# A 512-token, two-block transformer kernel: the first block's mixer run in two passes, tiles 0 and 1 ahead of the expert gather, tiles 2 and 3 between the gathered rows

## The reference, cut to what matters

```python
# first block
hn = rms_norm(h, norm_mix_g);  proj = hn @ w_in          # xv, bg, cg, ga, gg, 512 columns each
y_sc = bg * causal_conv(cg * xv, w[3])                   # 3 taps
y_cf = silu(layer_norm(causal_conv(ga * sigmoid(gg), w[31]) + b, ln_g, ln_b))   # 31 taps
h = h + concat(rms_norm(y_sc), rms_norm(y_cf)) @ w_out
hn = rms_norm(h, norm_ffn_g)
q = hn @ w_q                                             # 8 heads x 2 halves x 128
s1, s2 = q halves @ sub_keys;  top 16 of each, top 16 of their 256 sums -> idx, gates
u_sel = u[idx];  v_sel = v[idx]                          # 8 heads x 16 = 128 rows a token
h = rms_norm(h + sum(gelu(u_sel . hn) * gates * v_sel))
# second block: x = x + ffn1; x = x + attention mix; x = x + ffn2
```

## Time and profile before

| | |
|---|---|
| time, median of 3 runs | 2445.37 us (2444.99 to 2446.51) |
| span of the profiled execution, first to last instruction | 2440.3 us |
| busy share: PE, DVE, ACT, POOL | 87%, 75%, 48%, 31% |
| mean granted TensorE clock | 0.940 |
| moved by DMA | 760.89 MB, mean 312 GB/s |
| first and last gather issued | 243.09 us, 1807.03 us |

### The profile page before, as it was taken

The page is one execution under the profiler, slowest core; times in us unless marked ns, Lnnn a source line. Parts: engine busy times, 40 slices in busy tenths (PEclk is TensorE's granted clock), DMA queues, the critical chain, the costliest instruction groups (busy, mean ns, idle before and its releaser), DMA issues. The chain is left out here.

```text
span 2440.3 us, 28668 instructions
## 1 busy us (share of the span) xinstructions
PE 2117.7 (87%) x9528; PEld 1505.2 (62%) x9528; DVE 1829.9 (75%) x3369; ACT 1180.3 (48%) x3781; POOL 751.1 (31%) x634
## 2 busy tenths in 40 slices
PE   6987898897777776999784688699989999999999
PEld 6966444343222223885343467388539988898997
DVE  6985686777988888989889988866675656656664
ACT  5213556555666665343455555433344446445443
POOL 0000445445554554233456544433320001100000
PEclk9988899999999998999896679799999999999999
DMA  5211999999999999999999999999986444224454
GB/s 200 86 52 52 377 417 414 422 404 421 419 421 421 416 420 369 390 405 420 417 402 368 377 406 420 416 403 420 421 343 207 177 175 161 75 99 156 177 187 138
DMA packets 107460, 760.89 MB, mean 312 GB/s; under 512 B 12064, under 2 KB 12832, under 8 KB 16432
## 3 DMA queue, kind: packets, MB, share of 16 engines
q0 software_dynamic: 73728, 536.90, 53.9%
q1 hardware_dynamic: 33584, 222.15, 23.9%
HBM read 756.91 MB, written 2.10 MB: 311 GB/s over the span
## 5 line engine op out<-in xcount | busy, mean ns | idle before, releaser
L2448 POOL DMA_INDIRECT pair<-in_uv,idx x512 | 639.6, 1249 | 850.3 <-DVE resid L1079 519.5
L1837 ACT ACTIVATE smalls<-smalls 128x1 f32<-128x1 f32 (+1 forms) x2058 | 540.1, 286 | 640.5 <-DVE smalls L1747 622.3
L1747 DVE CUSTOM_DVE_ANT_0 pair<-pair,hn 128x1024 f32<-128x1024 f32 x512 | 624.2, 1221 | 179.8 <-DMA pair<-in_uv,idx 178.4
L596 PE MATMUL bank<-pair,diag 128*128 128x512 f32 x928 | 452.3, 619 | 124.5 <-ACT diag L1837 124.3
L596 PEld LDWEIGHTS bank<-pair,diag 128*128 128x128 f32 x928 | 167.3, 192 | 389.9 <-ACT diag L1837 243.9
L596 PE MATMUL bank<-ft,raw 128*128 128x256 f32 x1664 | 375.4, 389 | 11.9 <-DVE ft L1073 11.9
L596 PEld LDWEIGHTS bank<-ft,raw 128*128 128x128 f32 x1664 | 324.6, 196 | 58.7 <-issue 12.7
L1079 DVE SCALAR_TENSOR_TENSOR resid<-pair,smalls,resid 128x1024 f32<-128x1024 f32 x275 | 352.4, 1281 | 0.6 <-ACT smalls L1837 0.6
L1073 DVE TENSOR_TENSOR half<-raw,half 128x1024 fp32r<-128x1024 f32 (+1 forms) x204 | 235.6, 1194 | 124.6 <-ACT half L1837 123.2
L1837 ACT ACTIVATE half<-raw 128x1024 fp32r<-128x1024 f32 (+1 forms) x204 | 199.5, 1026 | 128.9 <-PE bank L596 128.8
L596 PE MATMUL bank<-ft_hi,half 128*128 128x256 f32 x960 | 178.4, 287 | 1.5 <-DVE ft_early L1073 1.5
(11 more groups left out here) (288 smaller groups left out, 2966.2 us busy)
## 6 DMA issues: line engine op xcount, KB each, us to landing
raw<-in_wts SPq DMA_DIRECT2D x196, 1024.0 KB
pair<-in_uv,idx POOLq DMA_INDIRECT x512
raw<-in_wts SPq DMA_DIRECT2D x10, 512.0 KB
raw<-in_wts SPq DMA_DIRECT2D x4, 720.0 KB
resid<-in_x SPq DMA_DIRECT2D x4, 512.0 KB, 6.3
out<-resid SPq DMA_DIRECT2D x8, 256.0 KB, 5.7
raw<-in_wts SPq DMA_DIRECT2D x2, 768.0 KB
rowt<-in_rows SPq DMA_DIRECT2D x1, 1076.0 KB, 12.6
```

Of the source, the lines that this page charges most:

```text
L596: return e.matmul(o, a, b, start=start, stop=stop)
L1747: e.tensor_tensor_reduce(b[:, 0:1024], b[:, 0:1024], HN[i // 128], 1.0, 0.0, ALU.mult, ALU.add, actv[:, i % 8:i % 8 + 1]).then_inc(dotted, 1)
L1837: return e.activation(o, i, f, **kw)
L2448: e.indirect_dma_start(pair[i % NPAIR], None, uv, bass.IndirectOffsetOnAxis(ap=idx[:, n % SLOTS, k:k + 1], axis=0)).then_inc(pairs_in[i % ...
```

## The change

The opening now runs for the meta tokens and tiles 0 and 1 alone. A second pass does tiles 2 and 3 between the gathered rows 0 and 136, with plain float matmuls on the raw chunks (no split). Its fourteen chunks are loaded a second time; `wout` of the first pass is loaded whole into four buffers of its own, unsplit. The score calls are cut in two, tiles 0 and 1 in rows 0 to 138 and tiles 2 and 3 in rows 148 to 244, which loads the eight chunks of `w_q` once more. All rows below 264 are added on PE. `REST_ROW` and `CALL_ROW` say at which row a chunk is worked on.

```diff
-CALLS = [(0, 0, 1), (1, 0, 1)] + [(h, 0, NT) for h in range(2, 8)] + [(0, 1, NT), (1, 1, NT)]
+CALLS = ([(0, 0, 1), (1, 0, 1)] + [(h, 0, 2) for h in range(2, 8)] + [(0, 1, 2), (1, 1, 2)]
+         + [(h, 2, 4) for h in range(8)])
+CALL_ROW = [16 * (c - 2) if c < 10 else 148 + 12 * (c - 10) for c in range(len(CALLS))]
+for _n, _key in enumerate([("cf2", i) for i in range(4)] + [("sc2", i) for i in range(4)] + [("bg2", i) for i in range(2)]):
+    REST_ROW[_key] = 20 + 16 * (_n // 2) + 6 * (_n % 2)
+REST_ROW.update({("wout2", 0): 100, ("wout2", 2): 108, ("wout2", 1): 116, ("wout2", 3): 121})
-ON_PE = [i < HALF + 8 and not (i < 128 and i % 4 == 3) or LAST_ON_PE <= i < PAIRS - 2 for i in range(PAIRS)]
+ON_PE = [i < HALF + 8 or LAST_ON_PE <= i < PAIRS - 2 for i in range(PAIRS)]
-for _k in [1] * 8 + [2] * 8 + [1, 2, 1, 2, 1] + [0] * 11:
+for _k in [1] * 10 + [2] * 6 + [1, 2, 1, 2, 1, 2] + [0] * 10:
@@ DVE, the taps of the first pass: two lanes, one for each tile
-            taps = [conv(acc[:, ct, :], upad, "cf", 31, ct, 16, ct + 1, taps_done) for ct in range(4)]
+                for t in range(2):
+                    lanes[t].append(conv(acc[:, ct, t * P:(t + 1) * P], upad, "cf", 31, ct, 16 + t * P, P, ct + 1, taps_done[t]))
-                pump(12 if ct else 11)
+                pump(14)
@@ DVE, ahead of route(0)
+            row_out(0)
+            y_mean("ms_sc", 1, 1, 2)
+            pump(999)
+            y_added("y_sc", 1, 3, 1)
+            centred("mean", 1, accs[1])
@@ DVE, behind route(0)
+            spread("var", 1, rstd[1])
+            inverted(rstd[1], 2)
+            levelled(accs[1], rstd[1])
+            y_mean("ms_cf", 1, 5, 6)
+            y_added("y_cf", 1, 4, 5)
+            mean_at(HN_NORM[1])
+            row_out(1)
@@ DVE, the taps of the second pass, 256 tokens wide
+                for two in ((0, 1), (2, 3)):
+                    pair_ = [conv(acc2[:, ct, :], upad2, "cf", 31, ct, 0, HALF, 9 + ct, taps_done[2]) for ct in two]
+                    for _ in range(30):
+                        for lane in pair_:
+                            yield 36 + step * 58 // 120
+                            next(lane)
+                            step += 1
@@ PE, one chunk of the second pass
+            def rest_projected(name, c):
+                r = REST_ROW[name, c]
+                w = raw_chunk((name, c), 8)
+                for j in range(2):
+                    o, done = fresh(name, 2 * c + j)
+                    for kt in range(8):
+                        ins = mm(o[:, 0:HALF], w[:, kt, j * P:(j + 1) * P], XR[:, kt, :], kt == 0, kt == 7)
+                        if kt % 4 == 3 and (j, kt) != (1, 7):
+                            yield r + 2 * j + kt // 4 + 1
@@ PE, the loop over the rows
             for i in range(LAST_ON_PE):
-                if i % 16 == 0:
-                    steps = scores_in_steps(i // 16 + 2) if i < 128 else iter(())
                 if ON_PE[i]:
                     add_row(i)
-                next(steps, None)
+                others.until(i)
+                calls.until(i)
```

More of the change, by code:

```diff
@@ new lines, in rest_out @@
+            def rest_out(stage, src, c, ready):
+                r = REST_ROW["wout2", c]
+                yield r
+                e.wait_ge(ready, 12)
+                w = raw_chunk(("wout2", c), 4)
+                for m in range(2):
+                    o, done = fresh(stage, c // 2 * 2 + m)
+                    for k in range(4):
+                        ins = mm(o[:], src[:, k, m * P:(m + 1) * P], w[:, k, :], k == 0, k == 3)
+                        if k % 2 == 1 and (m, k) != (1, 3):
+                            yield r + 2 * m + k // 2 + 1
+                    ins.then_inc(done, 1)
@@ L1148, in conv @@
                         ins.then_inc(v_step, vs_.up())
+                        done = vs_.n
                     yield
-            taps = [conv(acc[:, ct, :], upad, "cf", 31, ct, 16, ct + 1, taps_done) for ct in range(4)]
+            lanes = [[], []]
             def pump(n):
-                while n and taps:
-                    if next(taps[0], taps) is taps:
-                        taps.pop(0)
-                    else:
+                while n and (lanes[0] or lanes[1]):
+                    lane = (lanes[0] + lanes[1])[0]
+                    mine_ = lanes[0] if lane in lanes[0] else lanes[1]
+                    mine_.remove(lane)
+                    if next(lane, lane) is not lane:
+                        mine_.insert(1, lane)
@@ L1784, in vector @@
+            first, steps, others, taps = Paced(chain("A")), iter(()), Paced(rest()), Paced(rest_taps())
             for n in range(32):
@@ L1962, in normed @@
+            for t in range(2):
+                gained(ysc, "g_sc", halves[t], ysc_ok, 4)
             def normed(k, p, ready):
@@ L2329, in scalar, with scores_between @@
             gates(0)
-            for t in (2, 3):
-                row_squared(t)
-            for t in (2, 3):
-                row_turned(t)
-            scores(1)
-            first = Paced(chain("A"))
+            cf_rows(1)
+            all_added("y_cf", 1)
+            all_added("y_sc", 1)
+            row_squared(1)
+            row_turned(1)
+            def scores_between():
+                for c in range(2, 10):
+                    yield from scores_in_steps(c)
+                for t in (2, 3):
+                    yield 140 + 5 * (t - 2)
+                    filled(e, "q", 19)
+                    row_turned(t)
+                for c in range(10, len(CALLS)):
+                    yield from scores_in_steps(c)
@@ L2336, in scalar @@
+            first, calls, others = Paced(chain("A")), Paced(scores_between()), Paced(rest())
             for n in range(32):
-                steps = scores_in_steps(n + 2) if n < 8 else iter(())
                 for k in range(16):
```

848 lines of the change are left out of this document (514 added, 334 removed).

## The result

The changed kernel took 2436.06 us (median of 7 runs, 2431.34 to 2437.48) against 2444.99 for the kernel before on the same chip (7 runs, 2440.9 to 2448.21): a ratio of 0.997, 95% interval 0.9959 to 0.9981. It is faster by 0.3%. I had predicted 2452.4, slower by 0.3%; the time lies in the range of 2428 to 2479, but the sign was wrong. Part of the 2452.4 is not the change: I had put all of the 5.1 us between the span and the median down to what lies around the instructions, but every run on record takes 1.8 to 2.1 us more than its span, and the other 3 are the spread of the kernel before.

A forecast was written before the change was run, and what follows sets the result against it. The prediction took gathered rows as DMA-bound, the opening as bound otherwise, and PE as fullest in the second pass. Terms -80 + 3 + 35 + 17 + 22 + 10 = +7 us gave 2452.4 us, range 2428 to 2479.

The forecast's parts named there:

- The opening: Start to eighth gather: first gather at 158 us, eighth at 184 against 264.2, -80 us (bounds -70 and -90).
- the rival of a later opening: Opening: with lone-lane taps (0.38 us) it ends some 20 us later, result 2472; chance 0.12.
- the three middle terms: First, rows 7 to 138: +3, +35, +17 us; under DMA as the bound: +35, +17, +22, 74 in all.
- With 2% idle 251: Rows 20 to 100: PE's sum of 246 us becomes 251 with idle time, against 215.8 before: +35 us.
- with waits 99: Rows 100 to 131: PE's sum of 96 us becomes 99, against 82.1 before: +17 us.
- DVE waits some 3: Rows 0 to 20: DVE waits for the norms of tiles 2 and 3 behind row 3: +3 us.
- DMA as the bound: Rival: PE's load is hidden, only bytes count, 22 chunks at 2.53 make 56 us instead of 74; chance 0.25.
- my sum: Whole kernel: all terms added give +7 us, 2452.4 us; chance 0.37, own range 2444 to 2465.
- A sign that doesn't work: Second pass: DMA share under 1.0 would show PE as the bound; staying at 1.0 would refute the prediction.
- The routes: Rows 336 to 352: two routes of 8.7 us make DVE's stretch 68 us against 58.6: +10 us.
- the routes are hidden: Rival, rows 336 to 352: the routes cost nothing, 10 us less, 2442, no change; chance 0.11.
- The edge: Rows 20 to 131: the sum turns at 111 rows in 343 us, 3.09 a row; predicted 3.15.

The follow-up runs named there:

- e9: Changed kernel with the opening's taps 256 tokens wide, both tiles at once, one lane a channel block: 2440.54 us (one run).
- e2: Changed kernel loading 512 instead of 2048 columns of each of the 22 added chunks, all products made as before: 2427.24 us (one run).
- e3: Changed kernel with half the products of the second pass's ten w_in chunks left out, chunks loaded whole: 2428.31 us (one run).
- e6: Changed kernel with every eighth row from 20 to 128 (13 rows) added on DVE instead of PE: 2426.23 us (one run).
- e8: Changed kernel with first score call ahead of the column sum, routes in rows 128 to 160, 13 rows on DVE, rates early: 2409.36 us, ratio 0.9856.
- e1: Changed kernel with the two routes of rows 336 to 352 moved to the blocks of rows 256 and 288: 2432.73 us, ratio 0.9965.
- e5: Changed kernel with those two routes back in rows 128 to 160, score calls 11 rows apart instead of 12: 2426.5 us, ratio 0.9927.

## Why the prediction was wrong, point by point

**The opening held.** The timeline of DVE in the changed kernel, as in the earlier trace rows:

```profile
33.70 5.39 DVE L1183 SCALAR_TENSOR_TENSOR acc<-upad,colt,acc 128x128 f32<-128x128 f32 x14
...
84.93 3.32 DVE L1183 SCALAR_TENSOR_TENSOR acc<-upad,colt,acc 128x128 f32<-128x128 f32 x9
...
122.71 1.29 DVE L1183 SCALAR_TENSOR_TENSOR hn<-resid,smalls,rowt 128x1024 f32<-128x1024 f32 x1 [0.72 <-POOL smalls L2632]
123.98 11.63 DVE L1183 SCALAR_TENSOR_TENSOR acc<-upad,colt,acc 128x128 f32<-128x128 f32 x44
138.51 0.69 DVE L1177 TENSOR_TENSOR acc<-acc,bank 128x512 f32<-128x512 f32 x1 [1.57 <-PE bank L637]
144.81 0.29 DVE L1788 MAX8 vals<-scores 128x8 f32<-128x128 f32 x1 [5.61 <-ACT scores L2025]
```

The lone lane costs 5.39/14 = 0.385, the two lanes 11.63/44 = 0.264 (foretold 0.38 and 0.265). Tile 0's taps end at 88.2 (87.3), `hn` starts at 122.71 (122.6), the route at 144.81 (144.6), the gather goes out at 155.05, where the sum without hand-overs said 154.8. The 3 us that I had added for 25 hand-overs were not needed: over the whole way the small errors of the terms cancel. From first to eighth gather it took 26.92 (26). PE's first 48 products behind an idle stretch of 17.05 us took 7.66 us and the next 48 took 5.90 (8.4 and 5.6). The windows show the slow clock there: granted 0.50 (1.2 GHz) from 89.79 to 93.50 us, and 1.00 (2.4 GHz) from 98.09 on. The row that I had priced them by doesn't show it: the 48 products at 20.17 us of the kernel before, 8.68 us behind 5.07 idle, stand at a granted clock of 1.00, so what made them slow is open and my price for the new ones was right for a reason that this row doesn't give. So the rival of a later opening, with taps at the lone price throughout, fell. By shape, the 240 taps of 25 to 140 us show their own duration:

```profile
L1183 DVE SCALAR_TENSOR_TENSOR acc<-upad,colt,acc 128x128 f32<-128x128 f32 x240 | 67.2, 346 | 0.9
```

346 ns against the line's 354 and the 291 of the add formula in the Trainium skill ("VectorE: DVE Perf Modes", section on the TRN2 errata). Its advice on wide tiles holds for DVE's own time (51.2 us against 67.2), but e9 shows that here a step that way, to 256, cost 3.6 us.

**Where the sign went: rows 7 to 138.** The step that failed is the sizing of the three middle terms, "With 2% idle 251", "with waits 99" and "DVE waits some 3". The mechanism was right: e2 shows that bytes are not the bound from row 27 to 138, e3 that PE's products are it up to row 107, and in e6 fewer rows on PE took 2.1 us off rows 107 to 138 too. The three terms together were 13.3 us too dear, each on the side of slower. They failed in different ways. PE's groups by shape in rows 107 to 138 show two of them:

```profile
L637 PE MATMUL bank<-pair,diag 128*128 128x512 f32 x125 | 58.6, 596 | 4.2 <-ACT diag L2025 4.2
...
L637 PE MATMUL bank<-ht,raw 128*128 128x128 f32 x32 | 4.3, 277 | 0.0
```

From row 27 to 107, 5 of the 7.0 us are the idle time that I had added: PE was idle for 0.00 us. The other 2.2 are the bare sum, 246 against 243.79: I had priced all calls at 6.9, but the calls in rows 96 and 112 are for tile 1 alone (`(0, 1, 2)` and `(1, 1, 2)`), with products 128 wide instead of 256, which is 2.6 or 2.7 us less for each. From row 107 to 138 PE's work was 91.21 us and not 96, with the second such call in it (4.3 instead of 6.9) and smaller sums, and PE waited 4.2 us for ACT's diagonals, more than the 3 that I had added. That the stretch took 95.44, close to the bare 96, is luck. In rows 7 to 27 PE was busy 51.98 of 54.61 us; the norms of tiles 2 and 3 added 0.3 and not 3. That the seven gathers in flight hid them is how I read it. With the 2.3 of the opening the three terms make 15.6 us, in a result that is the difference of two sums of 80.

**DMA as the bound.** This rival was priced at 56 us for the three middle terms by bytes alone. They took 64.0. Of that, 6.7 is PE's excess above the floor that e3 found (243.79 - 237.08), and e8 took 2.3 more off rows 107 to 138 (95.44 - 93.15), where its rate was 411 GB/s; whether bytes bind at 93.15 no run shows. So the truth lay between my sum and the rival, nearer to the rival than I weighed it (0.25 against 0.37).

**A sign that doesn't work.** I wrote that the prediction is wrong if DMA share stays at 1.0 in the second pass. It stayed at 1.00 and PE was the bound all the same. The share counts busy time of the DMA engines, and e2 took 7% of the traffic away and moved it by 0.01. GB/s tells: 421 when DMA sets the pace (e3, e8), 419 in e6, 410 and 381 when PE does. The Trainium skill ("Perfetto Trace Analysis", section "Identifying the Most-Contended Engine") calls the occupancy of DMA engines misleading and asks for the utilization of the HBM instead; the trace agrees. For TensorE the same section does not trust the busy share of matmuls and asks, beside the share of peak arithmetic, for the busy share of weight loads. Here the rows differ: weight loads were at 155.29 of 243.79, 64%, in the stretch where e3 showed PE as the bound, and the matmul share, 100%, was the one that told.

**The routes.** Rows 336 to 352 took 68.02, as foretold (68). Of the 2.7 us over my 10 for rows 251 to 359, 2.4 lie in the seven rows behind it. That the routes are hidden is refuted by e1 and e5.

**Rows 138 to 251** took 22.6 more (22 foretold), eight chunks at the price of a row and 2 ahead of them. The number held; that it is the bytes alone is not shown, since e2 took three quarters of these bytes away and won only 8.0 us. Behind row 359 I foretold nothing, and the 5.5 us measured there are spread and one execution, as said above.

**What would have told.** The edge: 111 rows in 343 us was where my sum turned. They took 339.2 (243.79 + 95.44). I had named the edge, 7 us from my own 350, and gave the side beyond it 0.30. With bare sums, 246 + 96 = 342 for these rows (the second of them right by luck), +0 for rows 7 to 27 and 155 for the first gather, the change comes to 7 - 8 - 3 - 3 = -7: faster by 0.3%.

## What to carry over

Where two engines read full in one stretch, compare the GB/s with that of a stretch that is surely bound by DMA, with transfers of the same size; if it is lower, DMA is not the bound, whatever its share says. When a forecast is a small difference of large terms, read the width of every call that is priced, add the bare sums of rows and keep the margins for the range: margins that all point one way decide the sign. And work that was moved into a stretch where DMA is full cost about its bytes (22.6 us against 20 for eight chunks) until an engine passed the time of the bytes; there, put back just enough on the next engine (here 13 rows) to stay under.

## What the runs showed of the hardware

- PE ran 243.79 of 243.79 us at a granted clock of 1.00 beside DMA at 410 GB/s, 3% under the 421 that e3 reached with PE at 92%.
- 128-wide operations on DVE that wait for the one before start every 0.385 us, two independent lanes every 0.264; at 256 wide a lone lane takes 0.52 and two in turn 0.40 each. Twice the width costs 0.13 to 0.14 us a tap, alone or in turn.
- The same 32 products 128 wide took 3.73 us right behind other work and 5.23 to 5.36 behind an idle stretch of 7.84 or 3.41 us. The granted clock was 1.00 (2.4 GHz throughout) in the first and 0.69 and 0.68 (partly 1.2 GHz) in the others. A column sum of eight took 1.13 behind 3.41 us of idle time and 2.05 behind 7.84.
- A table load on ACT takes 1.28 us, and the next activation starts 0.01 us behind it. In the timeline of ACT:

```profile
151.69 1.28 ACT L2025 ACT_TABLE_LOAD   x1
152.98 0.31 ACT L2025 ACTIVATE gat<-gat,sm 128x16 f32<-128x16 f32 x1
```
